# Cached keys and values split and turned beside the first 16 attention jobs, the sample's jobs behind tile 2, three masks made one operation per job

## The reference

```
xn = rms_norm(x); q, k, v, qi, ki, wi, u, vs = split(xn @ w_in)      # q, k, qi, ki rotary
score  = sum_h relu(qi_h . ki) * wi_h;  not admissible -> -inf        # chunk-causal, CHUNK 64
top_val, top_idx = top_k(score, 256)
logits = q . k[top_idx] / 8;  p = softmax(logits);  attn = p @ v[top_idx]   # 8 heads x 64
sgu    = gelu(u) * (W_s @ layer_norm(gelu(vs)) + b_s)
h = x + concat(attn, sgu) @ w_out
y = rms_norm(h + (silu(rms_norm(h) @ w_gate) * (rms_norm(h) @ w_up)) @ w_down)
```

## Time and profile before

| | us |
|---|---|
| median of 3 runs (1465.62 to 1471.02) | 1467.63 |
| the profiled execution | 1470.07 |
| its span in the trace | 1468.1 |
| PE busy / DVE / ACT / POOL in the span | 1288.5 / 827.8 / 717.2 / 444.4 |
| mean granted share of TensorE's clock | 0.947 |

### The profile page before, as it was taken

One profiled execution on the slowest core, in us unless ns is written; L12 is line 12 of the kernel. 1 busy time (PEld: TensorE's weight loads), 2 busy tenths in 40 slices (PEclk: granted clock), 3 DMA queues, 4 the chain that ended last, 5 costly groups with the idle time before them and its releaser, 6 DMA issues.

```text
span 1468.1 us, 29504 instructions
## 1 busy us (share of the span) xinstructions
PE 1288.5 (88%) x10636; PEld 927.3 (63%) x10636; DVE 827.8 (56%) x1512; ACT 717.2 (49%) x1408; POOL 444.4 (30%) x518
## 2 busy tenths in 40 slices
PE   5968887999995347788997999999999998999997
PEld 3443334544443225566454888888888887888887
DVE  4323675789988275997755655555555552212022
ACT  3545788888785524886333544444444442001011
POOL 4772436377279300000202333333333310000001
PEclk9987999999998578999998999999999999999999
DMA  5221000112111200101430222222222128121013
GB/s 192 87 63 32 15 13 34 58 45 79 58 31 31 77 1 16 58 17 59 138 115 29 59 57 57 57 57 57 57 57 57 29 79 212 44 79 37 0 30 90
DMA packets 81596, 86.69 MB, mean 59 GB/s; under 512 B 6768, under 2 KB 63120, under 8 KB 81520
## 3 DMA queue, kind: packets, MB, share of 16 engines
q1 hardware_dynamic: 76112, 75.07, 17.7%
q10 hardware_dynamic: 4848, 8.99, 1.6%
q0 software_dynamic: 560, 1.61, 0.4%
HBM read 72.34 MB, written 13.31 MB: 58 GB/s over the span
## 4 chain that ended last, share of the span: by engine, by line
PE 52%; DVE 8%; ACT 3%; issue 2%; POOL 2%; DMA 2%; SPq 1%; POOLq 0%; DVEq 0%; ACTq 0%
PE PS L1155 28%; PE PS L1212 14%; PE PS L1118 5%; DVE M L1891 2%; DVE M L1880 2%; PE PS L1015 1%; PE PS L1038 1%; PE PS L1068 1%; DMA M<-in_w_down 1%; SPq L647 1%; ACT M L1481 1%; PE PS L1199 1%; ACT M L1492 1%; PE PS L1132 0%; DVE M L1857 0%
## 5 line engine op out<-in xcount | busy, mean ns | idle before, releaser
L1155 PE MATMUL PS<-M 128*128 128x264 f16 x3696 | 420.7, 278 | 9.6 <-ACT M L1600 9.6
L1155 PEld LDWEIGHTS PS<-M 128*128 128x128 f16 x3696 | 363.3, 98 | 66.5 <-ACT M L1600 10.2
L889 PE MATMUL PS<-M 128*128 128x512 f16 (+1 forms) x1512 | 306.9, 364 | 3.6 <-DVE M L441 3.6
L1212 PE MATMUL PS<-M 128*128 128x256 f16 x2112 | 233.5, 274 | 5.9 <-DVE M L2113 5.9
L889 PEld LDWEIGHTS PS<-M 128*128 128x128 f16 (+1 forms) x1512 | 139.5, 103 | 154.2 <-issue 14.2
L1212 PEld LDWEIGHTS PS<-M 128*128 (+1 forms) x2112 | 207.3, 98 | 31.7 <-issue 6.8
L683 POOL TENSOR_TENSOR small<-small 128x1 f32<-128x1 f32 x27 | 5.5, 205 | 520.9 <-ACT M L1547 271.1
L1787 DVE TENSOR_SCALAR_CACHE_REDUCE M<-M,small 128x384 f16<-128x384 f32 (+5 forms) x162 | 132.9, 880 | 0.8
L837 POOL TENSOR_TENSOR M<-M 128x264 f32<-128x264 f32 x44 | 34.8, 791 | 283.1 <-ACT M L1600 283.1
L1952 DVE SCALAR_TENSOR_TENSOR M<-M 128x2048 f16<-128x2048 f32 (+1 forms) x44 | 89.0, 2025 | 36.2 <-ACT M L1538 36.2
L2113 DVE SCALAR_TENSOR_TENSOR M<-PS,M 128x256 f32 (+1 forms) x32 | 13.6, 424 | 165.7 <-PE PS L1212 165.6
(11 more groups left out here) (177 smaller groups left out, 1903.5 us busy)
## 6 DMA issues: line engine op xcount, KB each, us to landing
M<-in_w_in SPq DMA_DIRECT2D x24, 512.0 KB, 3.8
M<-in_w_gate SPq DMA_DIRECT2D x22, 512.0 KB, 4.1
M<-in_w_up SPq DMA_DIRECT2D x22, 512.0 KB, 5.2
M<-in_w_down SPq DMA_DIRECT2D x20, 512.0 KB, 3.9
M<-in_x_prompt SPq DMA_DIRECT2D x16, 512.0 KB, 4.8
M<-in_w_out SPq DMA_DIRECT2D x8, 512.0 KB, 3.8
h_scratch<-M ACTq DMA_DIRECT2D x8, 512.0 KB, 5.0
M<-h_scratch SPq DMA_DIRECT2D x16, 256.0 KB, 7.7
```

Source lines behind the costliest of these rows:

```text
L889: last = pe.matmul(bank(b)[:, 0:w], xnT[:, ds(t, 1), k, s, :].squeeze(1), wt[wbuf(c)][:, k * w:(k + 1) * w], start=(k == 0 and i == 0), st ...
L1155: last = pe.matmul(o, wsp[x][:, zw, wb, k * P:(k + 1) * P], ablk[:, ab, za, k * HT + s * SC:k * HT + (s + 1) * SC], start=(name not in kep ...
L1212: last = pe.matmul(o[:, 0:256], cols[:, ds(m * SC + r * P, P)], wt[dc % 2][:, f, :], start=(f == 0 and i == 0), stop=(f == FT - 1 and i == 2))
```

## The change

It moves work among the engines' streams and adds or removes no arithmetic.

- The q group takes no cached block any more. All sixteen blocks, now `cache_k` first (u = 0 to 7) and `cache_v` after it (u = 8 to 15), pass through three `kc32` buffers in turn (`kc_slot`).
- ScalarE casts blocks 0 and 1 at the end of the q group, between the last high part of q and the copies that follow it, and block j + 2 in attention job j, behind the copy of the turned block j (`cached_high`, `cached_turned`).
- GpSimd makes the low parts of blocks 0 and 1 before it clears the unused parts of the packed queries, the other fourteen after (`cached_low`).
- TensorE turns block j in attention job j, for j below 8 (`turn_cached`), between `qk(j + 3)` and `turn`.
- The sample's two jobs come after tile 2: `ATT_TILES = [0, 1, 2, LAST, 3, ...]`. The pieces of `w_out`, counted from there, go to jobs 28, 33, ..., 63.
- The three late masks are cut into their 21 operations, one before the peak in each of the jobs 0 to 20 (`mask_step`). Their scratch rows lie in parts of the probability buffers that tiles 0 to 2 do not use.

```diff
-ATT_TILES = [0, 1, LAST] + list(range(2, LAST))
+ATT_TILES = [0, 1, 2, LAST] + list(range(3, LAST))
...
         def kc_slot(u):
-            return u % 2 if u < 8 else (u - 8) % 3
+            return u % 3
...
-        MASK_JOBS = {2 * i + 1: EARLY_MASKS + i for i in range(NS - EARLY_MASKS)}
...
-                src = a["cache_v" if u < 8 else "cache_k"][0, 0].rearrange("s h d -> s (h d)")
+                src = a["cache_k" if u < 8 else "cache_v"][0, 0].rearrange("s h d -> s (h d)")
...
                     lagged(not_vs(B), c, t, rep, 1)
-                    if NAMES[c] == "q" and not (isinstance(t, int) and t == 0):
-                        pool.wait_ge(kc_hi, t)
-                        v = Vs[:, ds(t - 1, 1)].squeeze(1)
-                        pool.tensor_tensor(v[:, :, 1, :], heads(kc32[(rep - 1) % 2]), v[:, :, 0, :],
-                                           ALU.subtract).then_inc(kc_lo, 1)
...
+            def cached_low(u):
+                pool.wait_ge(kc_hi, u + 1)
+                v = kchl[u % 2] if u < 8 else Vs[:, u - 8]
+                pool.tensor_tensor(v[:, :, 1, :], heads(kc32[kc_slot(u)]), v[:, :, 0, :],
+                                   ALU.subtract).then_inc(kc_lo, 1)
+
+            cached_low(0)
+            cached_low(1)
             pool.wait_ge(post_evac, n_unit(NC - 1, LAST) + 2)
...
+            for u in range(2, 16):
+                cached_low(u)
...
-            for i in range(8):
-                pe.wait_ge(kc_lo, 8 + i + 1)
+            def turn_cached(i):
+                pe.wait_ge(kc_lo, i + 1)
                 if i >= 2:
                     pe.wait_ge(kc_evac, i - 1)
...
             for j in range(NJ):
                 if j + 3 < NJ:
                     qk(j + 3)
+                if j < 8:
+                    turn_cached(j)
...
+            def cached_high(u):
+                act.wait_ge(kc_loaded[kc_slot(u)], 16 * kc_loads(u))
+                if 2 <= u < 8:
+                    act.wait_ge(kc_turned, u - 1)
+                out = kchl[u % 2] if u < 8 else Vs[:, u - 8]
+                act.activation(out[:, :, 0, :], heads(kc32[kc_slot(u)]), ACT.Copy).then_inc(kc_hi, 1)
...
                     flush(H, c, 1)
+                    if c == NC - 1:
+                        cached_high(0)
+                        cached_high(1)
                     flush(ST, c, 1)
...
                 if j + 2 < NJ:
                     exp(j + 2)
+                if j < 8:
+                    cached_turned(j)
+                if j + 2 < 16:
+                    cached_high(j + 2)
...
             for j in range(NJ):
-                if j in MASK_JOBS:
-                    mask(MASK_JOBS[j])
+                if j < 7 * (NS - EARLY_MASKS):
+                    mask_step(EARLY_MASKS + j // 7, j % 7)
```

More of the change, by code:

```diff
@@ L1450, in step @@
                     lagged(R, c, t, rep, 2)
-                    if NAMES[c] == "q" and not (isinstance(t, int) and t == 0):
-                        act.wait_ge(kc_loaded[(rep - 1) % 2], ((t - 1) // 2 + 1) * 16)
-                        act.activation(Vs[:, ds(t - 1, 1), :, 0, :].squeeze(1), heads(kc32[(rep - 1) % 2]),
-                                       ACT.Copy).then_inc(kc_hi, 1)
                     if searching(c, t):
@@ L1845, in _, with mask_step @@
             link(dve.scalar_tensor_tensor(out=sure, in0=fix, scalar=STEP, in1=sure, op0=ALU.mult, op1=ALU.add))
-            def mask(j):
+            mask_made = {}
+            def mask_step(j, k):
                 t = SCORE_TILES[j]
@@ L1858, in mask @@
-                link(dve.scalar_tensor_tensor(out=eq, in0=rank, scalar=need[:, j:j + 1], in1=eq, op0=ALU.is_le,
-                                              op1=ALU.mult))
-                link(dve.scalar_tensor_tensor(out=sc, in0=sc, scalar=kth[:, j:j + 1], in1=eq, op0=ALU.is_gt,
-                                              op1=ALU.add))
-                link(dve.tensor_scalar(sc, sc, -1.0, -NEG, ALU.add, ALU.mult))
-                if t == LAST:
-                    dve.memset(scores[:, SC_OFF[LAST] + TOK:SC_OFF[LAST] + NT * P], NEG).then_inc(mask_ready, 1)
+                eq, rank = (x[:, 0:S] for x in tie[j >= EARLY_MASKS])
@@ new lines, in mask_step @@
+                dve.wait_ge(sel, n_sel[0])
+                if k == 0:
+                    ins = dve.tensor_scalar(rank, sc, kth[:, j:j + 1], None, ALU.is_gt, ALU.add,
+                                            accum_out=cnt[:, j:j + 1])
+                elif k == 1:
+                    ins = dve.tensor_scalar(eq, sc, kth[:, j:j + 1], None, ALU.is_equal)
+                elif k == 2:
+                    ins = dve.tensor_scalar(need[:, j:j + 1], cnt[:, j:j + 1], -1.0, float(TOPK), ALU.mult, ALU.add)
+                elif k == 3:
+                    ins = dve.tensor_tensor_scan(rank, eq, eq, 0.0, ALU.add, ALU.max)
+                elif k == 4:
+                    ins = dve.scalar_tensor_tensor(out=eq, in0=rank, scalar=need[:, j:j + 1], in1=eq, op0=ALU.is_le,
+                                                   op1=ALU.mult)
+                elif k == 5:
+                    ins = dve.scalar_tensor_tensor(out=sc, in0=sc, scalar=kth[:, j:j + 1], in1=eq, op0=ALU.is_gt,
+                                                   op1=ALU.add)
+                else:
+                    ins = dve.tensor_scalar(sc, sc, -1.0, -NEG, ALU.add, ALU.mult)
@@ L1867, in peak @@
+                ins.then_inc(sel, 1)
+                n_sel[0] += 1
+                if k == 6:
+                    mask_made[t] = n_sel[0]
+                    if t == LAST:
+                        dve.memset(scores[:, SC_OFF[LAST] + TOK:SC_OFF[LAST] + NT * P], NEG).then_inc(mask_ready, 1)
             def peak(j):
@@ L1912, in _ @@
             for i in range(EARLY_MASKS):
-                mask(i)
+                for k in range(7):
+                    mask_step(i, k)
             dve.wait_ge(post_evac, n_unit(NC - 1, LAST) + 2)
```

23 lines of the change are left out of this document (3 added, 20 removed).

## The result

| | before | after |
|---|---|---|
| median, us (4 runs each) | 1466.62 (1462.77 to 1471.02) | 1450.06 (1449.19 to 1453.96) |
| the profiled execution, us | 1470.07 | 1450.45 |
| its span, us | 1468.1 | 1448.4 |
| mean granted share of TensorE's clock | 0.947 | 0.958 |

The ratio is 0.9891, with a 95% interval of 0.9857 to 0.9925: 1.1% faster. The forecast was 1446 for the time and 1448.3 for the profiled execution.

The account below looks back on a forecast made before the run. VectorE was taken to bound attention wherever it is not waiting for keys or packs. Terms: -23 + 1.2 = -22, profiled execution 1470.07 to 1448.3, 1445.8 us for the time; range 1434 to 1458.

Parts of the forecast that it names:

- q without the cached blocks: q group: eight low parts leave GpSimd's stream, 7.0 us a step in steps 4 to 8; -6.4 us.
- Two casts on the path: End of q: two casts between the last high part and the second copies add 1.14 us.
- Cached keys out of the gap: Between q and attention: first `qk` directly follows q's last copy, -18.1 us, standing at 477.8.
- Jobs 0 to 20: First attention jobs with masks and cached blocks: 53 us in sum, first packed `qk` at about 531.
- the ring: Three load buffers in jobs 0 to 13: 6.9 us for three blocks, block 14 at 511.
- rival 4: Cached loads: only two blocks in flight, 3.5 us a block, +13 us; chance 0.06.
- The packs behind tile 2: Packed jobs keep their wait, beside tile 3's jobs instead of tile 2's; tile 4's first peak at 576.
- rival 1: TensorE's clock: thinly busy before the packs, so packed `qk` take twice as long; 10 us, 1456; chance 0.10.
- The pieces behind tile 4: Pieces of `w_out`: six instead of five behind tile 4's first peak, +1.2 us.
- Rival 2: Jobs 0 to 13: each of 14 low parts costs VectorE its whole 1.15 us; +9, 1455; chance 0.09.
- Rival 5: Job loop loses its lead of two jobs, each paying its block's whole path; about 1519 us; chance 0.03.
- Rival 3: First jobs: masks and jobs fit without ring waits, 46 us instead of 53; 1438 us; chance 0.12.

Follow-up runs that it names:

- e7: The changed kernel with cache_v split in the q group again, only cache_k beside the first jobs; 1452.69 us, ratio 0.9908.
- e9: The changed kernel with two load buffers for the cached blocks instead of three; 1451.68 us, ratio 0.9881.
- e10: The changed kernel with the three late masks whole again, before the peaks of jobs 1, 3 and 5; 1459.27 us, ratio 0.9927.
- e3: The changed kernel with the pieces of w_out every 4 jobs (28, 32, ..., 56) instead of every 5; 1449.76 us, ratio 0.9882.
- e2: The changed kernel with six masks ahead of the first peak, only the last one cut into jobs 0 to 6; 1446.40 us, ratio 0.9851.
- e5: The changed kernel with four of the eight pieces of w_out beside the packs and just behind them; 1443.53 us, ratio 0.9822.
- e4: The changed kernel with the sixteen cached low parts cleared instead of computed, so GpSimd does not read beside the masks; 1446.62 us, ratio 0.9858.
- e1: The kernel before with all seven masks made ahead of the first peak, nothing else changed; 1446.22 us, ratio 0.9864.
- e11: The changed kernel with cache_k back in the gap beside most mask work, cache_v in the jobs, old tile order, pieces moved earlier; 1439.43 us, ratio 0.9793.

## Why the prediction was right, and where not

The forecast of 1446 lies 4 us below the median, and the direction, the place and the main gain were right: closing the gap gave 18.1, and the masks and blocks fitted into the jobs, 4.1 us shorter up to tile 4's first peak. That the sum fits is in part luck: against the forecast the q group was 4.1 worse and the pieces 4.4, the first jobs 2.5 better and the packs 1.8, and 1.9 came from a shorter start that the change has no part in. By steps:

1. *q without the cached blocks: mis-sized.* Steps 4 to 8 won 3.75 where I had 4.9 (7.28 a step, forecast 7.0). Steps 0 to 3, from which I took 1.5 for ScalarE's casts, won nothing: 27.9 instead of 27.25 (405.46 to 433.36). There the search rounds that ScalarE shares fill it whether the casts are there or not; that is argued, no run took the rounds away. The last rotary, in which an operation takes 2.23 beside VectorE's last early mask (1.98 in the earlier trace rows), grew from 5.7 to 6.5, which I did not see coming. Since e7 lengthens q by 4.3 and shortens the jobs by 3.6, the low parts did not vanish, they moved.

2. *Two casts on the path: right.* The casts stand at 471.22 with 1.13, and the second copy of q's low part follows directly: +1.04.

3. *Cached keys out of the gap: right.* 18.7 became 0.6. The first `qk` stands at 480.06 for a forecast of 477.8: q won 4.1 less than forecast, and the start was 1.9 shorter.

4. *Jobs 0 to 20: the stage right within 3 us, its reason half wrong.* I had 53 from a ring of three loads at 6.9 and from VectorE, together. It took 50.5 from the first `qk` on (50.0 from the first peak), and the ring had no part in it: I had taken a load at 4.42, the one that the chain showed, as the duration of every load, and the loads here landed in 2.6 at the median (2.5 to 4.4). The block 14 cast came at 511.2, as forecast, but because ScalarE and VectorE set the pace. e9 shows it from the other side. So rival 4 was as far from the truth as the step that it amplified. VectorE's work was 45.20 in 50.50 with 4.6 of collisions in it, so about 40.7 of its own against my 45, and collisions of 4.6 against my 2: the two errors nearly cancel. The rest of the stage, 5 us, is the waits at the start and for ScalarE's `pt_cast`. That cutting the masks matters, 9 us by e10, stood in no step; I had taken it as given.

5. *The packs behind tile 2: right.* 43.2 us from packed `qk` to tile 4's first peak, forecast 45. Two things of rival 1 show: the first packed `qk` took 4.84 at a rising clock, and the clock was 0.97 in the mean of that stretch (0.82 for the earlier trace rows), so the packs, which lay at half clock in part before, now gained it back. Rival 1 did not come: TensorE was granted 0.67 in the first jobs, where it was 0.57, and no `pv` took more than 3.32.

6. *The pieces behind tile 4: wrong by count.* Before, tile 4's first peak was at 599.12 and the pieces at 606.5, 619.6, 631.6, 645.2 and 660.0 came behind it, five. In the change they are at jobs 28 to 63, and all but the one at 566.80 come behind 573.76: seven, not the six that I counted, since I placed tile 4's first peak at its own job and not three jobs ahead, where VectorE issues it. By tile, from first peak to first peak:

   | us | before | after | pieces in it, before and after |
   |---|---|---|---|
   | tile 4 | 17.4 | 19.9 | 1, 2 |
   | tile 5 | 21.0 | 21.4 | 2, 1 |
   | tile 6 | 21.2 | 22.2 | 1, 2 |
   | tile 7, to the output projection | 29.8 | 31.6 | 1, 2 |

   A piece costs more than its own 1.23 where nothing covers TensorE's wait for the `pt_low` behind it. In tile 7 that is the last one, at 661.40 (a wait of 2.09, 1.8 in the stretch; e3, whose last piece comes earlier, has 29.9 there). In tile 4 TensorE waits 2.12 before 580.50 and 2.17 before 593.36, where before no wait behind tile 4's first peak was longer than 1.64. Tile 5 is longer with a piece fewer, because the granted clock fell to half from 593.6 to 597.0, right behind the second of these waits:

```profile
593.36 0.85 PE L1036 MATMUL PS<-ident,M 128*128 128x128 f32 x4 [2.17 <-DVE M L1907]
```

e2 and e5, with the same single piece and no such fall in tile 5, have 20.2 there, so it costs 1.2. It is no accident of one run: in all eight traces with the packs behind tile 2 the clock falls once behind tile 4's first peak, in tile 4 or 5, and in none of the five with the old order. Why it fell there and not behind the wait at 580.50 is open.

**Rival 2**, the collision of GpSimd's low parts with VectorE, was real, and I had taken its size from the wrong quantity. The Trainium skill (SBUF — State Buffer, Who interferes with whom) says that a VectorE instruction with two SBUF inputs and a GpSimd instruction that reads SBUF shut each other out. The trace agrees, in kind and in size: the later of the two lost what was left of the earlier one, less 0.1 to 0.2 us (e4). The same section counts `tensor_scalar`, but not the form that also writes out its accumulator, among the operations that can take the shared ports with one input, and the trace agrees there too: the operation of 0.68 in e4 took 1.30 in the change, and the count of 1024 columns 1.27 in both. The rule does not give 16 us, though. That sum charges VectorE with the whole 1.15 of all fourteen low parts; in the trace four of them had to wait themselves, and the others were partly over when a VectorE operation came, or met operations that read PSUM. `peak` and `pt_low`, which do, kept their 0.29 beside a low part (488.14 against 488.02 to 489.17), as I had argued against the rival.

**Rival 5**, the loop that loses its lead, did not come: the exponentials waited for VectorE's peaks alone, 2.4 at the longest and 10.6 in sum. **Rival 3**, 46 us for the stage, was 4.5 too short, where my 53.2 was 2.7 too long.

What the prediction missed altogether is the alternative. I read that VectorE idles for 30.55 us ahead of its first peak and is the bound in the jobs behind it, and accepted that the gap be closed at 18.1. That VectorE's own late work fits into that gap (e1) follows from the same two rows: 23.5 us of masks on one side, 30.55 idle on the other.

## What to carry to other kernels

Where the engine that bounds a stage idles ahead of it, first look for work of its own that fits into the idle time: one constant did as much here as rebuilding five streams, and filling the gap and closing only the rest (e11) did 30 us against 17. A table of places that is counted from a landmark moves with the landmark, so after moving one, count again how many land in the stage without slack, and from the point at which the engine issues and not from the job's number. Where two engines shut each other out, the price is what is left of the instruction under way, so add up the overlaps and not the durations. For a ring of buffers take the median load, and for a bound that a single row gives, ask how many rows of that kind there are.

## What the runs showed of the hardware

- A VectorE scan over 896 fp16 columns takes 2.02 us alone and 2.70 where it starts beside a GpSimd subtraction over 512 columns with 0.82 left to run. That subtraction takes 1.15 alone, 2.00 where it starts beside that scan with 1.05 left to run, and 2.97 beside a scan with 2.02 left. Whichever starts first keeps its time; the other is held for what is left of it, less 0.1 to 0.2 us.
- A VectorE tensor-scalar operation with one input in SBUF (896 columns, float32 to float16) went from 0.68 to 1.30 beside the same GpSimd operation. The masked count (L1858) of 1024 columns took 1.27 both beside GpSimd and without, and operations that read PSUM kept their time.
- A memset of the same 512 columns on GpSimd takes 0.52 and slows none of VectorE's operations: in e4 one at 503.55 lies inside the scan of 1024 columns, which takes 2.28 there.
- TensorE's granted clock fell to half once behind tile 4's first peak in each of the eight traces with the packs behind tile 2, in seven of them within 0.5 us of the end of a wait of 2.1 to 2.2 us, and in none of the five others, where no wait there was longer than 1.64.
- A load of one cached block of 256 KB lands in 2.6 us at the median with up to three in flight, and in 4.4 at worst.
